# One decoder layer on one core: a new attention stage, and the output product to routing in the order tile 0, tile 1, samples

## What is computed

```python
proj = x @ w_in                                  # 1024 -> 3072: q, k, v of both groups
o    = attention per head, ALiBi, softmax        # prompt: causal; samples: 256 cached + 4 new keys
o    = head_rmsnorm(o) * gn                      # mean of squares over the 64 features of a head
hx   = layer_norm(ALPHA * x + o @ w_out)
top4 = top_k(hx @ w_router + b_router)           # of 32 experts
hx   = layer_norm(ALPHA * hx + sum of gates * expert(hx))   # clamped SwiGLU, w_gate_up, w_down
```

## Time and profile before

| | before |
|---|---|
| median of 3 runs | 1241.05 us (1238.41 to 1243.55) |
| profiled execution | 1237.81 us, its span 1235.9 us |
| busy share of the span | PE 94%, DVE 22%, ACT 15%, POOL 3% |
| granted TensorE clock, mean | 0.972 |
| DMA | 454.38 MB, mean 368 GB/s |
| chain that ended last | PE 74%, DMA 20%, DVE 2%, ACT 2% |

### The profile page before, as it was taken

How to read it: one execution, slowest core, us unless ns; L and a number is a source line. 1 busy time by engine, 2 the same in 40 slices (tenths; PEclk the granted TensorE clock), 3 DMA queues, 4 the chain that set the end, 5 groups by cost and what they waited for, 6 DMA issues and landing times.

```text
span 1235.9 us, 14419 instructions
## 1 busy us (share of the span) xinstructions
PE 1163.2 (94%) x5485; PEld 473.8 (38%) x5486; DVE 270.3 (22%) x656; ACT 185.8 (15%) x457; POOL 39.0 (3%) x71
## 2 busy tenths in 40 slices
PE   7999876979999999999999999999999999999996
PEld 4777653343333333333333333333332323232322
DVE  1023455251303121212203030212121211203023
ACT  0123432121111010102011110101020201010101
POOL 0120300010000000000000000000000000000000
PEclk9999898887999999999999999999999999999998
DMA  8881575942999999999999999999999999999993
GB/s 288 322 304 52 193 265 185 375 183 102 391 384 428 427 427 428 428 428 427 428 428 428 428 428 428 428 428 427 428 428 428 427 428 428 428 428 428 420 413 133
DMA packets 83078, 454.38 MB, mean 368 GB/s; under 512 B 7098, under 2 KB 19778, under 8 KB 35810
## 3 DMA queue, kind: packets, MB, share of 16 engines
q1 hardware_dynamic: 80720, 440.44, 86.3%
q0 software_dynamic: 1728, 10.75, 2.4%
q10 hardware_dynamic: 594, 2.73, 0.6%
HBM read 450.36 MB, written 11.93 MB: 374 GB/s over the span
## 4 chain that ended last, share of the span: by engine, by line
PE 74%; DMA 20%; DVE 2%; ACT 2%; issue 1%; SPq 1%; POOL 0%; DVEq 0%; ACTq 0%
PE bank L891 22%; PE bank L933 17%; DMA ring<-in_w_gate_up 15%; PE bank L870 8%; PE bank L640 8%; PE bank L606 5%; PE bank L778 3%; PE bank L958 3%; DMA ring<-in_w_down 2%; PE bank L1009 1%; PE bank L728 1%; PE bank L971 1%; ACT xtok L1116 1%; ACT actT L1116 1%; DMA out<-kstage 1%
## 5 line engine op out<-in xcount | busy, mean ns | idle before, releaser
L891 PE MATMUL bank<-ring,xg 128*64 128x512 f32 x1904 | 419.4, 596 | 10.4 <-DMA ring<-in_w_gate_up 10.4
L891 PEld LDWEIGHTS bank<-ring,xg 128*64 128x64 f32 x1904 | 133.3, 137 | 287.5 <-issue 262.4
L933 PE MATMUL bank<-ring,actT 128*64 128x512 f32 x960 | 215.9, 597 | 3.8 <-ACT actT L1116 3.8
L1581 DVE TENSOR_TENSOR acc<-acc,bank 128x512 f32<-128x512 f32 x60 | 41.3, 688 | 493.6 <-PE bank L958 493.6
L933 PEld LDWEIGHTS bank<-ring,actT 128*64 128x64 f32 x960 | 66.6, 137 | 121.5 <-issue 118.7
L1242 ACT ACTIVATE sig<-gate 128x256 f32<-128x256 f32 x64 | 26.6, 416 | 526.2 <-DVE gate L1563 526.2
L870 PE MATMUL bank<-hx,pick 128*128 128x512 f32 (+1 forms) x192 | 100.4, 650 | 1.1 <-DVE pick L1547 1.1
L640 PE MATMUL bank<-xT,wblk 128*128 128x288 f32 x384 | 98.4, 414 | 0.6 <-DVE xT L1329 0.6
L640 PEld LDWEIGHTS bank<-xT,wblk 128*128 128x128 f32 x384 | 72.9, 193 | 20.0 <-DVE xT L1329 0.7
L1563 DVE TENSOR_SCALAR gate<-bank 128x256 f32<-128x256 f32 x64 | 26.9, 420 | 185.4 <-PE bank L891 165.1
L870 PEld LDWEIGHTS bank<-hx,pick 128*128 128x128 f32 (+1 forms) x192 | 32.2, 194 | 68.2 <-issue 67.0
(11 more groups left out here) (203 smaller groups left out, 697.1 us busy)
## 6 DMA issues: line engine op xcount, KB each, us to landing
ring<-in_w_gate_up SPq DMA_DIRECT2D x119, 2048.0 KB, 25.4
ring<-in_w_down SPq DMA_DIRECT2D x63, 2048.0 KB, 27.7
ring<-in_w_gate_up SPq DMA_DIRECT2D x16, 1024.0 KB, 18.4
wblk<-in_w_in SPq DMA_DIRECT2D x12, 1024.0 KB, 8.5
kring<-in_cache_k_moba SPq DMA_DIRECT2D x16, 256.0 KB, 4.5
out<-in_state_k_win POOLq DMA_DIRECT2D x8, 512.0 KB, 5.9
out<-in_state_v_win POOLq DMA_DIRECT2D x8, 512.0 KB, 6.4
vring<-in_cache_v_moba SPq DMA_DIRECT2D x16, 256.0 KB, 6.3
```

The costliest lines, as they stand in the source:

```text
L891: ins = nc.tensor.matmul(bank[n][64 * e:64 * e + 64, :], xg[:, k, 64 * e:64 * e + 64], w[:, 2048 * e + 512 * n:2048 * e + 512 * n + 512], ...
L933: ins = nc.tensor.matmul(bank[4 + half][64 * e:64 * e + 64, :], actT[:, j, 64 * e:64 * e + 64], w[:, at:at + 512], start=(j == 0), stop=(j ...
L1581: V.tensor_tensor(o, o, new, ALU.add).then_inc(S.added, 1)
```

## The change

What it does, part by part:

- **x** has a semaphore per tile and is turned tile by tile into all eight banks; VectorE and ScalarE share the copies. The identity is loaded ahead of the other constants.
- **Blocks by group, values by token.** The order is q, k, q, k, v, v of group 0 and the same of group 1 (`BLOCKS`), with three buffers instead of four. q and k are made as before; for v the operands are swapped, so that 128 tokens are rows and 256 features columns, and `turn_kv` of the values is gone. The samples' values take 16 matmuls of 32 rows in slots 11 and 23.
- **Two heads per step.** A step scores two heads at partitions 0 to 63 and 64 to 127, and four tables (`SCORE`, `TURN`, `MIX`, `KEY`, ...) say in which slot each piece runs. Keys of the samples are turned from slot 1 on, into six buffers.
- **Outputs by features.** The probabilities are divided before they are turned (`head_scale`), and `head_mix` gives features as rows, so `otok` and 16 of the 20 late transpositions are gone. The mean of squares over a head is now a matmul with `blk64` (a block matrix of 1/64), `mean_squares`; its root and reciprocal are wide tiles (`msq`, `root_means`, `scale_out`).
- **Output product** begins in slots 24 to 28 with features 0 to 511 (`out_part`), and is finished afterwards for tile 0, tile 1, then the samples. Logits are made with tokens as rows. `keep_warm` adds nine matmuls whose result is not used. The samples' LayerNorm is made on VectorE alone.
- **SyncE's order** of loads is new, as are the waits in it.

```diff
+    BLOCKS = [(g, kind, half) for g in range(2) for kind, half in ((0, 0), (1, 0), (0, 1), (1, 1), (2, 0), (2, 1))]
+    SLOTS_P, STEPS = 2 * len(BLOCKS), 29
+    SCORE = {4: 0, 6: 1, 8: 2, 10: 3, 16: 4, 18: 5, 20: 6, 22: 7}
+    TURN = {s + 1: n for s, n in SCORE.items()}
+    MIX = {11: 0, 13: 1, 15: 2, 17: 3, 22: 4, 24: 5, 25: 6, 26: 7}
+    MSQ = {12: 0, 14: 1, 16: 2, 18: 3, 23: 4, 25: 5, 26: 6, 27: 7}
+    KEY = {1: 0, 2: 1, 3: 2, 4: 3, 5: 4, 6: 5, 10: 6, 11: 7, 13: 8, 15: 9, 16: 10, 17: 11, 19: 12, 20: 13, 21: 14, 22: 15}
+    KROWS = {8: 0, 12: 1, 14: 2, 25: 3, 26: 4, 27: 5}
+    SAMP_SCORE, SAMP_TURN = {9: 0, 12: 1, 20: 2, 23: 3}, {10: 0, 13: 1, 21: 2, 24: 3}
+    SAMP_MIX = {14: 0, 18: 1, 24: 2, 26: 3}
...
+        load_v(0)
+        sp.dma_start(wrt[:, :, :], w_router[0].rearrange("(k p) e -> p k e", p=128)).then_inc(S.router_in, 16)
+        sp.dma_start(brt[:, :], b_router[0:1, :].broadcast_to([128, E])).then_inc(S.router_in, 16)
+
+        def free_slot(m):
+            return [s for s, n in KEY.items() if n == m - KRING][0]
+
+        for slot in range(1, SLOTS_P):
+            for n in range(3, len(BLOCKS)):
+                if 2 * (n - 3) + (3 if BLOCKS[n - 3][1:] == (2, 0) else 1) == slot:
+                    load_w_in(n)
+            if slot == 19:
+                sp.wait_ge(S.projected, 20)
+                load_wout(0)
+            for m in range(KRING, 16):
+                if free_slot(m) == slot:
+                    load_k(m)
+            if slot in (14, 18):
+                load_v(SAMP_MIX[slot] + 1)
...
+        load_unit(0, 0, 2)
+        sp.wait_ge(S.samp_mixed, 3)
+        load_unit(0, 0, 1)
...
+        sp.wait_ge(S.probs_turned, 16)
+        sp.wait_ge(S.head_mixed, 5)
+        load_unit(0, 0, 0, first, S.first_in)
         sp.wait_ge(S.samp_mixed, 4)
+        load_unit(0, 0, 6)
+        sp.wait_ge(S.head_mixed, 8)
+        sp.dma_start(bdn[:, :], b_down[0]).then_inc(S.bdn_in, 16)
+        sp.wait_ge(S.msq_done, 8)
+        load_unit(0, 0, 3)
...
+        def project(slot):
+
+            b, c = divmod(slot, 2)
+            g, kind, half = BLOCKS[b]
+            if c == 0:
+                pe.wait_ge(w_landed[b % 3], 16 * (b // 3 + 1))
+            if slot >= 2:
+                pe.wait_ge(*evacuated(slot - 2))
+            out, w = bank[slot % 2], wblk[:, b % 3]
...
+                if kind < 2:
+                    ins = nc.tensor.matmul(out[:, 0:T], w[:, k, 128 * c:128 * c + 128], xT[:, k, :],
+                                           start=(k == 0), stop=(k == KC - 1))
+                else:
+                    ins = nc.tensor.matmul(out[:, 0:256], xT[:, k, 128 * c:128 * c + 128], w[:, k, :],
+                                           start=(k == 0), stop=(k == KC - 1))
+            if kind == 2 and half == 1 and c == 1:
+                for k in range(KC):
+                    for n, blk in enumerate((b - 1, b)):
+                        ins = nc.tensor.matmul(out[NS * n:NS * n + NS, 256:512], xT[:, k, SEQ:T], wblk[:, blk % 3, k, :],
+                                               start=(k == 0), stop=(k == KC - 1), tile_position=(0, NS * n))
+            ins.then_inc(S.projected, 1)
+
+        def mean_squares(n):
+            pe.wait_ge(S.out_taken, n + 1)
+            if n == 0:
+                pe.wait_ge(S.blk_in, 16)
+            nc.tensor.matmul(bank[mix_bank(n)][:, 256:512], blk64[:, :], square[:, :], start=True,
+                             stop=True).then_inc(S.msq_done, 1)
...
+        def head_scores(n):
+            g, j = divmod(n, 4)
+            pe.wait_ge(S.proj_copied, copied_at(slot_of_tile(g, 1, j)))
+            if n:
+                pe.wait_ge(S.probs_copied, 2 * n)
+            for part in range(2):
+                for r in range(2):
+                    rows = slice(64 * r, 64 * r + 64)
+                    q, k = qkT[rows, 8 * g + j, :], qkT[rows, 8 * g + 4 + j, :]
+                    if part == 0:
+                        nc.tensor.matmul(bank[2 + r][:, 0:256], q[:, 128:256], k[:, 0:256], start=True, stop=True)
+                    else:
+                        nc.tensor.matmul(bank[2 + r][:, 256:384], q[:, 0:128], k[:, 0:128], start=True,
+                                         stop=True).then_inc(S.head_scored, 1)
...
+        def head_turn(n):
+            for r in range(2):
+                pe.wait_ge(S.head_scaled, 2 * n + r + 1)
+                for c, at in enumerate((256, 0, 128)):
+                    ins = turn(bank[2 + r][:, 128 * c:128 * c + 128], headS[:, r, at:at + 128])
+                ins.then_inc(S.probs_turned, 1)
...
+            out, P = bank[mix_bank(n)], headPT[n % 4]
+            for part in range(2):
+                for r in range(2):
+                    v = vtok[:, part, g, 64 * (2 * j + r):64 * (2 * j + r) + 64]
+                    rows = slice(64 * r, 64 * r + 64)
+                    if part == 0:
+                        nc.tensor.matmul(out[rows, 0:256], v, P[:, r, 0:256], start=True, stop=False)
+                    else:
+                        ins = nc.tensor.matmul(out[rows, 128:256], v, P[:, r, 256:384], start=False, stop=True)
+            ins.then_inc(S.head_mixed, 1)
...
+        def out_part(step):
+
+            if step == 24:
+                pe.wait_ge(S.outT_ready, 1)
+                pe.wait_ge(S.vtok_ready, v_at(23))
+                pe.wait_ge(wout_in[0], 16)
+                out_first(0, (0, 1))
+            if step == 25:
+                pe.wait_ge(wout_in[1], 16)
+                out_first(0, (2, 3))
+            if step == 26:
+                pe.wait_ge(S.probs_copied, 16)
+                out_first(1, (0, 1))
+            if step == 27:
+                out_first(1, (2, 3))
+            if step == 28:
+                pe.wait_ge(S.outT_scaled, 1)
+                pe.wait_ge(S.kstage_ready, 6)
+                out_first(2, range(4))
+
+        for slot in range(STEPS):
+            if slot < SLOTS_P:
                 project(slot)
+            else:
+                out_part(slot)
...
-            if slot in kv_slot:
-                turn_kv(kv_slot.index(slot))
-            s = slot - STEP0
-            keys = keys_at(s)
-            if 0 <= s < 2 * H:
-                head_scores(s)
-            if quad_at(s, 2) is not None:
-                samp_scores(quad_at(s, 2))
-            if keys:
-                turn_keys(keys[0])
-            if 1 <= s <= 2 * H:
-                head_turn(s - 1)
-            if keys:
-                turn_keys(keys[1])
-            if 2 <= s <= 2 * H + 1:
-                head_mix(s - 2)
-            if quad_at(s, 4) is not None:
-                samp_mix(quad_at(s, 4))
-            if quad_at(s, 3) is not None:
-                samp_turn(quad_at(s, 3))
...
-        pe.wait_ge(S.outT_scaled, 1)
-        out_product(2)
-        pe.wait_ge(S.outT_ready, KC)
-        out_product(0, stages(0))
-        out_product(1, stages(1))
-        for stage in stages(2):
-            stage()
-
+            ins.then_inc(S.routed, 1)
+
+        def keep_warm(n, tiles_done):
+            pe.wait_ge(S.hx_varied, tiles_done)
+            for _ in range(n):
+                nc.tensor.matmul(bank[2][:, :], ident, keep[:, 0:512], start=True, stop=True)
+
+        pe.wait_ge(wout_in[2], 16)
+        pe.wait_ge(wout_in[3], 16)
+        pe.wait_ge(S.outT_ready, 3)
+        for half in range(2):
+            for k in range(4, KC):
+                ins = out_product(0, half, k)
+            ins.then_inc(S.attended, 1)
+        for half in range(2):
+            for k in range(4, KC):
+                ins = out_product(1, half, k)
+            ins.then_inc(S.attended, 1)
+        turn_hx(0)
+        pe.wait_ge(S.outT_scaled, 2)
+        for k in range(4, KC):
+            for half in range(2):
+                ins = out_product(2, half, k)
+        ins.then_inc(S.attended, 1)
+        logits_product(0)
+        keep_warm(2, 2)
+        turn_hx(1)
+        logits_product(1)
+        keep_warm(3, 3)
+        turn_hx(2)
+        logits_product(2)
+        keep_warm(3, 3)
...
-            g, h = divmod(n, H)
-            s = n % 2
-            link(V.scalar_tensor_tensor(headB[:, s, :], att[:, A_DIST:A_DIST + 384], -SLOPES[h],
-                                        att[:, A_MASK + 384 * g:A_MASK + 384 * g + 384], ALU.mult, ALU.add))
-            dve.wait_ge(S.head_scored, n + 1)
-            if n >= 2:
-                dve.wait_ge(S.head_exped, 2 * n - 2)
-            V.scalar_tensor_tensor(headS[:, s, :], bank[s][:, 0:384], SCALE, headB[:, s, :],
-                                   ALU.mult, ALU.add).then_inc(S.head_summed, 1)
-            dve.wait_ge(S.head_summed, n + 1)
-            for t, cols in ((0, slice(256, 384)), (1, slice(0, 256))):
-                V.tensor_reduce(s_(c_max + 2 * n + t), headS[:, s, cols], AXX, ALU.max, negate=True).then_inc(S.head_maxed, 1)
...
+        def head_scale(n):
+            for r in range(2):
+                c = 4 * n + 2 * r
```

(106 more changed lines are left out.)

849 lines of the change are left out of this document (410 added, 439 removed).

## The result

The changed kernel takes **1199.4 us** (median of 4 runs, 1195.26 to 1200.91), 0.9655 of the time before (95% interval 0.9621 to 0.9689; before, in the same comparison, 1242.18). The forecast was 1215, the range 1197 to 1232.

A forecast was written before the change was run, and what follows sets the result against it. Expert loads at 427 GB/s bound the end, so unit 9's issue counts: 12.5 + 192.6 + 7.3 + 5.2 + 4 = 221.6, then to 278.2, 26.2 earlier; 1237.8 becomes 1211.6, plus 3.2 gives 1215 us, range 1197 to 1232.

The forecast's parts named there:

- What bounds the kernel: Expert stage, 361.5 to 1206.5 us, runs at the rate of the loads, 427 GB/s; the end hangs on the stream's start.
- Unit 9: First load of an expert unit that waits for expert matmuls; issue forecast at 278.2 us instead of 304.44, 26.2 earlier.
- The start: First projection put at 10.3 us instead of 15.7; with a first tile 2.2 us slower, 12.5.
- TensorE's work in the slots: Projections, heads, keys, samples and early output product in 29 slots at full clock: 192.6 us.
- the bounds of 3.0 and 4.7: Cost in us of two heads beside a projection: 3.0 if scores overlap too, 4.7 if neither scores nor mixing does.
- Where VectorE is late: Wide reciprocals, 6.9 us for 1024 columns, make TensorE wait: 7.3 us in slots 20 and 21, 5.2 after slot 27.
- the 4 us for other waits: Added for waits among the 29 slots, such as a first key not landed or a store of `kstage`.
- After the slots: Product's second half 14.0 us, routing tail 25, gather and first inputs 10.5, two units 7.1.
- The rival on the clock: Half clock in the longer routing tail slows gather by 4.4 us, inputs and two units 2.5, logits and turns 1; 20%.
- Fewer waits: Wide reciprocals cost near a multiply (-11 us) and the scores overlap (-5 at most): about 1201 us; 22%.
- The clock falls: TensorE drops to half clock from the routing tail on: about 1223 us; 20%.
- The slower case: Blocks 3 to 11 of w_in each come 3.6 us too late on the one load queue: 1247 us; 6%.

The follow-up runs named there:

- the slowest and fastest experiment: Slowest: changed kernel with the 16 key jobs in bunches, 1212.49 us. Fastest: reciprocals per pair, samples' product before turning tile 0, six unused matmuls, 1182.0 us.
- the run with early reciprocals: Changed kernel with one reciprocal per pair of heads right behind the copy of its mean squares, and the root behind it: 1186.27 us, 0.9569 of before.

## Why the prediction was off, step by step

- **What bounds the kernel: right.** Unit 9 fixes the end, from before to the slowest and fastest experiment.
- **The start: right.** Projection at 10.37 (10.3 forecast), and the first two tiles cost 1.9 us over later ones (2.2).
- **TensorE's work in the slots: the step that failed.** The term was 2.2 + 192.6 = 194.8; the same pieces of the changed kernel, added by distance of starts, are 183.2. Projections 102.1 for 99.6 (1.7 of it half clock), product 17.7 for 17.5, samples 21.6 for 23.2, k rows 3.2 for 3.9. But eight pairs of heads cost 22.8, not 28.8 (scores 0.85, turning 0.71, mixing 0.80, mean squares 0.48, together 2.85, below the lower bound of 3.0), and 16 key jobs 14.9, not 20.8. For heads I took 3.6 between the bounds of 3.0 and 4.7; the scores do run side by side, and that put the price at, and a little below, the lower bound. For keys the price was "1.09 and a gap", 1.3 in all, read at 191.00, where TensorE waited for a copy before the next job. But the row's 1.09 already holds an end that overlaps the next start. Where a job of before stands without a wait, the distance of starts was 156.68 - 155.75 = 0.93, the price that it has now:

```profile
155.75 1.09 PE L606 MATMUL bank<-keep,kring 128*128 128x128 f32 x8
156.68 0.49 PE L606 MATMUL bank<-keep,headP 128*128 128x128 f32 x3
```

- **Where VectorE is late: right in place and cause, a little too long.** The reciprocal took 6.55 us (6.9 forecast), 3.34 (3.5); TensorE waited 3.38 and 1.97 in slots 20 and 21 (3.2 and 4.1), and 3.67 at the end (5.2). Of the 4 us for other waits only 0.77 came, that for ScalarE's copy into `kstage`. Together 9.8 for 16.5. With the 11.6 of the work that is 18.2 us: the product's second half began at 203.36, not 221.6.
- **After the slots: too short.** 16.83 for 14.0, 27.1 for 25, 18.4 for 17.6, 62.3 us for 56.6. I had the clock at 1.00 from the product to the gather; it was 0.83 and 0.87. The missing step is the same each time: after a stretch in which it waited or worked in part, TensorE runs at half clock for some microseconds, although it is then busy throughout. The rival on the clock had that for the routing and behind it, not for the product. The rows of before show it too: from 295.20 to 304.40 TensorE is busy throughout, at 0.77. The changed kernel's clock in three such places:

```profile
145.00:147.00 2.00, 2.00 (x6) 1.58 (x5) 1.82 (x6) 1.17 (x7) 0.00 (x0) 0.50 0.01 4
...
205.00:207.00 2.00, 2.00 (x4) 0.77 (x3) 0.00 (x0) 0.00 (x0) 0.00 (x0) 0.50 0.57 239
...
236.00:238.00 2.00, 2.00 (x3) 0.88 (x3) 1.75 (x10) 0.00 (x0) 0.00 (x0) 0.50 1.02 426
```

- **The sum.** 5.7 - 18.2 = -12.5, unit 9 at 265.69 for 278.2. The median lay 0.7 us above its profiled execution, where I had added 3.2; that is most of the rest of 1215 - 1199.4 = 15.6. The miss ahead of the product, 18.2 us, was larger than that of the whole, and the 5.7 us too few behind it hid a part: that the sum came out this near is luck to that extent.
- **The rivals.** "Fewer waits" had the number, by luck. Of its reasons the scores side by side hold, worth 5.2 us of TensorE's time; the cheap wide reciprocal does not: taking it away gains 14.7. "The clock falls" was wrong for the gather (6.00) and right elsewhere: 1.3 us for the logits of tile 1, 1.7 behind the gather. The slower case, a w_in block too late, did not occur: after the first block, no load holds a projection.

The Trainium skill, in VectorE: DVE Perf Modes, First, the fixed hardware budget, gives a reciprocal a repeat count of 8, from which with 1.12 ns a column I had estimated 9.2 us for 1024 columns; 6.55 was measured, and 1.22 for a multiply of as many, a factor of 5.4.

Open is how long the clock stays low after a wait: the same tail had 0.86 in one trace and 0.94 in two others with the same code there, and I have not separated what decides it. How much of the unused matmuls' 0.6 and 1.1 us is worth and how much chance stays open too.

## What to carry to other kernels

Price small TensorE pieces by the distance of starts inside a packed stretch, not by their rows' length plus a gap. A wait on a short chain costs its idle time and can cost some microseconds of half clock on whatever comes next: 8 us of idle less were worth 13 to 15 with the reciprocals, while 9 us more, without the early half, cost 9. Put a slow operation where its engine is idle between projections, piece by piece, instead of once where the next engine wants the result. Matmuls that only hold the clock delay the next needed one if they outlast the slack ahead of it, and here the medians show no clear gain from them; look at the trace before keeping them.

## What was not expected of the hardware

- A reciprocal of 1024 columns takes 6.55 us, of 512 3.34, of 256 1.75 (in the run with early reciprocals): each further column costs 6.2 to 6.3 ns, nearly the 6.6 between the 155 and 354 ns of 2 and 32 columns.
- The six records of three unused matmuls of 512 columns took 2.82 to 2.84 us at clock 1.00 and 4.52 to 4.85 where it had fallen (0.50 to 0.73 in windows of 2 us): they slow down with the clock that they are to hold, and VectorE waited 1.53 us for the logits behind the 4.52.
- The scores of two heads at partitions 0 to 63 and 64 to 127, two matmuls of 256 and two of 128 columns, cost 0.85 us, and 1.50 when both lie in one half.
